# Halo tokens read channel-major, normalised without transposes, in a hybrid attention and pooling layer on eight cores

## What is computed

```python
h = rms_norm(x, norm_gain)                       # x * rsqrt(mean(x*x)) * gain
q, k, v, z_attn, u_pool, z_pool, gates = split(h @ w_in)      # 2048 x 16384
# attention: 3 groups of 8 heads, (window, dilation) = (128,1), (512,4), (2048,16)
#   q, k normalised per head, rope on 32 of 128 dims, softmax in the dilated window,
#   groups mixed by their softmax denominators
y_attn = (attn * silu(z_attn)) @ w_branch_attn
# pooling: trailing means over 2, 4, 8, 16 tokens minus the token, a map per group
y_pool = (pool * silu(z_pool)) @ w_branch_pool
out = x + (sigmoid(g_attn) * y_attn + sigmoid(g_pool) * y_pool) @ w_out
```

## Time and profile before

| | us |
|---|---|
| median of three runs | 1601.21 (1600.38 to 1602.24) |
| the execution with the profile | 1585.82 |
| its span, slowest core (6) | 1584.3 |
| spans of the eight cores | 1573.4 to 1584.3 |

### The profile page before, as it was taken

One profiled execution on the slowest core, in us unless ns is written; L12 is line 12 of the kernel. 1 busy time (PEld: TensorE's weight loads), 2 busy tenths in 40 slices (PEclk: granted clock), 3 DMA queues, 4 the chain that ended last, 5 costly groups with the idle time before them and its releaser, 6 DMA issues.

```text
span 1584.3 us, 27008 instructions; the slowest of 8 cores (1573.4 to 1584.3 us)
## 1 busy us (share of the span) xinstructions
PE 1549.4 (98%) x10200; PEld 934.9 (59%) x10200; DVE 640.2 (40%) x839; ACT 602.4 (38%) x985; POOL 86.9 (5%) x168
## 2 busy tenths in 40 slices
PE   6899999999999999999999999999999999999998
PEld 4555668746874846848656864856544444444443
DVE  5677723165514445543165515454522111113221
ACT  4566535353434543455353435553641111110000
POOL 0000000000000000000000000000000101000000
PEclk9989999999999999999999999999999999999999
DMA  9798441123131143241123131143544565542893
GB/s 244 185 237 209 97 90 32 28 51 73 33 54 34 35 75 71 38 78 32 28 52 73 32 54 34 35 86 61 123 77 85 105 106 98 89 80 40 189 224 120
DMA packets 42929, 138.04 MB, mean 87 GB/s; under 512 B 7025, under 2 KB 8049, under 8 KB 39537
## 3 DMA queue, kind: packets, MB, share of 16 engines
q0 software_dynamic: 23552, 85.58, 32.1%
q1 hardware_dynamic: 14498, 42.29, 8.4%
q10 hardware_dynamic: 4752, 8.44, 1.9%
HBM read 206.86 MB, written 10.49 MB: 137 GB/s over the span
## 4 chain that ended last, share of the span: by engine, by line
PE 93%; DMA 3%; DVE 2%; ACT 1%; issue 1%; SPq 0%; DVEq 0%; ACTq 0%; POOLq 0%
PE p_pp L464 77%; PE p_pnd L464 6%; PE p_psc L464 5%; PE p_pS L464 4%; DMA s_xt<-xh 1%; DMA pt_spill<-s_pt 1%; DMA s_wr<-w_in 1%; PE p_pnd L568 1%; DVE s_ub L475 1%; ACT s_xn L545 0%; ACT s_rr L468 0%; DVE s_xn L479 0%; DVE s_hTo L574 0%; DVE s_aT L479 0%; ACT s_hTh L472 0%
## 5 line engine op out<-in xcount | busy, mean ns | idle before, releaser
L464 PE MATMUL p_pp<-s_hTo,s_wr 128*128 128x512 bf16 (+4 forms) x3616 | 769.7, 367 | 9.5 <-DMA s_wr<-w_in 5.3
L464 PEld LDWEIGHTS p_pp<-s_hTo,s_wr 128*128 128x128 bf16 x3616 | 343.6, 99 | 370.9 <-issue 26.6
L479 DVE SCALAR_TENSOR_TENSOR s_kS<-p_pp,s_cst,s_rr 128x512 bf16<-128x512 f32 (+1 forms) x96 | 94.7, 986 | 273.4 <-ACT s_rr L468 267.4
L464 PE MATMUL p_pp<-s_wr,s_hTo 128*128 128x256 bf16 x1536 | 175.4, 273 | 0.0
L464 PEld LDWEIGHTS p_pp<-s_wr,s_hTo 128*128 128x128 bf16 x1536 | 160.7, 118 | 6.4
L464 PE MATMUL p_pp<-s_wr,s_hTh 128*128 128x256 bf16 x1344 | 159.5, 273 | 0.0
L464 PE MATMUL p_pp<-s_hTh,s_wr 128*128 128x512 bf16 (+1 forms) x768 | 155.7, 353 | 0.0
L468 ACT ACTIVATE s_rr<-p_pS 128x512 f32<-128x512 f32 x144 | 83.6, 580 | 181.5 <-PE p_pS L464 174.1
L464 PEld LDWEIGHTS p_pp<-s_wr,s_hTh 128*128 128x128 bf16 x1344 | 145.3, 136 | 1.9
L468 ACT ACTIVATE s_rr<-s_rr 128x512 f32<-128x512 f32 x208 | 128.5, 618 | 19.1 <-ACT s_rr L468 0.4
L487 POOL DMA_DIRECT2D s_wr<-w_in x128 | 67.6, 529 | 1219.2 <-PE p_pp L464 764.0
(11 more groups left out here) (75 smaller groups left out, 1205.0 us busy)
## 6 DMA issues: line engine op xcount, KB each, us to landing
s_wr<-w_in POOLq DMA_DIRECT2D x128, 512.0 KB, 5.5
s_xt<-xh SPq DMA_DIRECT2D x23, 1024.0 KB, 10.8
s_wr<-w_y POOLq DMA_DIRECT2D x16, 512.0 KB, 5.5
s_wo<-w_out POOLq DMA_DIRECT2D x16, 512.0 KB, 8.6
s_xr<-xh ACTq DMA_DIRECT2D x32, 256.0 KB, 7.8
out<-s_ob SPq DMA_DIRECT2D x32, 256.0 KB, 6.5
pt_spill<-s_pt SPq DMA_DIRECT2D x8, 256.0 KB, 6.6
s_pT<-pt_spill SPq DMA_DIRECT2D x1, 2048.0 KB, 12.9
```

Source lines behind the costliest of these rows:

```text
L464: S.op("pe", lambda t: t.matmul(out, lhsT=lhsT, rhs=rhs, start=start, stop=stop), reads=reads, writes=writes, cost=n / 2400.0 + 0.0025)
L479: S.op("dve", lambda v: v.scalar_tensor_tensor(out=out, in0=in0, scalar=scalar, in1=in1, op0=op0, op1=op1), reads=reads, writes=writes, co ...
```

## The change

The host also hands over the halo with channels on the partitions (`xg`: 20 pieces, each 128 channels x 4 x 384 tokens in f32, 768 KB). The tokens before 1920 are treated in five groups of 384 (`H_T0`: 1536 first, then 0, 384, 768, 1152). For a group (`h_task`) 16 squares of 384 columns are made on ScalarE, 15 adds of 384 columns in f32 on GpSimd bring them to one tile `acc`, one f32 matmul against ones (`onesf`) sums over the partitions and leaves the sum in all of them, Ln and Exp on ScalarE make the scale `rb`, and 16 products of 384 columns on VectorE (x times gain's column, times `rb`) write `hTh`. The tile-wise halo tasks, with their 240 transposes and 30 copies, are gone.

The first group must be done before the first V; the other four may go on beside the first V and the first K and Q (`end_halo`). For this the SBUF zones are laid out anew: the tiles that the first attention unit takes lie behind the x pieces. The masks and the third part of the rope table are loaded in `end_halo`, the other two parts where the whole table was. Weight blocks are issued up to three blocks ahead (`prefetch`), since GpSimd's queue now also has adds in it. The planner gets one modelled DMA channel of 290 GB/s for all large transfers, and per task its own margin and the engines whose lateness counts. The x loads of the own tokens stay as they were.

```diff
@@ -94,8 +97,11 @@
                 at = max(at, d.end + 0.1)
         if o.isdma:
             self.T[eng] = at + 0.1
-            self.chan[eng] = max(self.chan[eng], at + 1.5) + kb / (270.0 if kb >= 1024 else 540.0)
-            o.end = self.chan[eng] + 0.7
+            if kb >= 512:
+                self.bulk = max(self.bulk, at + 1.5) + kb / 290.0
+                o.end = self.bulk + 0.7
+            else:
+                o.end = at + 2.2 + kb / 540.0
         else:
             self.T[eng] = at + cost
             o.end = at + cost + (0.25 if eng == "pe" else 0.05)
...
@@ -205,10 +211,12 @@
 
 
 class Cond:
-    __slots__ = ("reads", "writes", "rings", "after", "heavy")
-
-    def __init__(self, reads=(), writes=(), rings=(), after=(), heavy=0.0):
+    __slots__ = ("reads", "writes", "rings", "after", "heavy", "margin", "on")
+
+    def __init__(self, reads=(), writes=(), rings=(), after=(), heavy=0.0, margin=0.6, on=("dve", "act")):
         self.heavy = heavy
...
@@ -282,9 +289,9 @@
                     self.step(t)
                     break
             else:
-                late = max(T["dve"], T["act"]) - T["pe"]
                 for t in self.live:
-                    if t.cond.heavy and late <= t.cond.heavy and self.ready(t):
+                    c = t.cond
+                    if c.heavy and max(T[e] for e in c.on) - T["pe"] <= max(c.heavy, self.floor) and self.ready(t):
                         self.step(t)
                         break
                 else:
...
+        zq_end = zQ.at
         xn_t = [zA.put(f"xn{i}", [128, D], BF16) for i in range(2)]
         gb = zA.put("gb", [128, D], F32)
         UW = PRE + TOWN
         grow = place("gr", [1, D], F32, at=aT_at)
         onef = place("of", [1, 128], F32, at=aT_at + 4 * D)
         uext0 = [zA.put(f"ua{i}", [128, UW], F32) for i in range(2)]
-        xt_t.append(place("xt3", [128, D], F32, at=zA.at))
...
@@ -488,8 +505,24 @@
                 "p (k c) -> p k c", k=KC)), behind=behind, writes=[B_wr[i]], dsem=f"dw{i}", kb=1024)
             return i
 
-        def load_wblock(col0, behind=()):
-            return load_w(w_in, col0, behind)
+        G0 = SEQ_G[0][0] * 1024
+        plan = ([CU, CU + 128, CZP, CZP + 128]
+                + [c + 256 * q + 128 * i for q in (1, 2, 3) for c in (CU, CZP) for i in (0, 1)]
+                + [CV + G0, CV + G0 + 128, CK + G0, CQ + G0, CK + G0 + 128, CQ + G0 + 128])
+        issued, taken = [], [0]
+
+        def prefetch(upto, behind=()):
+            while len(issued) < min(upto, len(plan)):
+                issued.append(load_w(w_in, plan[len(issued)], behind))
+
+        def load_wblock(col0, ahead=3):
+            n = taken[0]
+            taken[0] += 1
+            if n >= len(plan):
+                return load_w(w_in, col0)
+            assert plan[n] == col0
+            prefetch(n + ahead + 1)
+            return issued[n]
 
         B_gr, B_of = Buf("gr"), Buf("of")
         S.op("sp", lambda s: s.dma_start(out=grow[:], in_=gain), writes=[B_gr], dsem="dc1", kb=8)
...
+
+        load_early([x_op[0]])
+        load_early([x_op[1]])
+
+        XLATE = (5.0, 2.0, 2.0, 2.0, 2.0)
+        B_xq = [Buf(f"xq{i}") for i in range(6)]
+        XQ = (3, 2, 0, 1, 4, 5)
+        nq = [0]
+
+        def issue_q():
+            q = nq[0]
+            if q == 20:
+                return
+            nq[0] += 1
+            i = XQ[q % 6]
+            S.op("sp", lambda s: s.dma_start(out=xq_t[i][:], in_=xg[q * 128:(q + 1) * 128, :].rearrange(
+                "p (k t) -> p k t", k=4)), writes=[B_xq[i]], dsem=f"dq{i}", kb=8 * HT // 4)
+
         tp_t = [p[:, :].bitcast(BF16) for p in pnd_t]
 
         slot = {}
...
-            if j < 9:
-                slot[j] = xn.take("x")
+            slot[j] = xn.take("x")
             xi, ni, c0 = loaded[j], slot[j], 3 * j
             stt(xn_t[ni][:], xt_t[xi][:], stat[:, c0 + 2:c0 + 3], gb[:], ALU.mult, ALU.mult, 2048,
                 [xt.B[xi], B_st[j], B_gb] + bx, [xn.B[ni]], cost=2.35)
             if bx:
                 inherit(xt.B[xi], bx)
-            nx = j + 4 if j < 7 else j + 3
-            if j != 7 and nx < 24:
-                issue_x(nx)
+            if j < 5:
+                issue_x(j + 4)
+            if j == 6:
+                inherit(B_xq[3], [xt.B[2]])
+                inherit(B_xq[2], [xt.B[1], xt.B[2]])
+                issue_q()
+                issue_q()
+            if j == 8:
+                inherit(B_xq[0], [xt.B[0]])
+                inherit(B_xq[1], [xt.B[0], xt.B[1]])
+                issue_q()
+                issue_q()
 
         def x_turn(j, half):
...
@@ -583,35 +640,55 @@
                 vcopy(hTh[:, ks, THALO - 128:THALO - 16], i_ap[:, :, 16:128], 896, [pnd.B[pi]], [B_hH[15]])
             pnd.free(pi)
 
-        def x_task(j):
-            ti = tiles[j][1]
+        sf = Ring(sf_t, "sf")
+        B_acc, B_rb, B_of2 = Buf("acc"), Buf("rb"), Buf("onesf")
+
+        def padd(out, in0, in1, n, reads, writes):
+            S.op("pool", lambda g: g.tensor_tensor(out=out, in0=in0, in1=in1, op=ALU.add), reads=reads,
+                 writes=writes, cost=0.1 + n * 0.0022)
+
+        def h_task(gi):
+            t0 = H_T0[gi]
+            Bh = [B_hH[t0 // 128 + t] for t in range(HT // 128)]
 
             def gen(me):
-                yield Cond(after=[tile_front[j - 1]])
-                yield Cond(reads=[xt.B[loaded[j]]], rings=[xn], heavy=XLATE)
-                x_square(j, [])
-                x_scale(j, [])
-                xn.owner[slot[j]] = me
-                tile_front[j].done = True
-                for half in range(2):
-                    yield Cond(reads=[xn.B[slot[j]], B_id], rings=[pnd], heavy=XLATE)
-                    pi = x_turn(j, half)
-                    ks = slice(half * 8, half * 8 + 8)
-                    o_ap = hTh[:, ks, ti * 128:ti * 128 + 128]
-                    i_ap = tp_t[pi].rearrange("p (k c) -> p k c", c=128)
-                    if half == 0:
-                        acopy(o_ap, i_ap, 1024, [pnd.B[pi]], [B_hH[ti]])
+                yield Cond(after=[h_front[gi - 1]] if gi else [])
+                for kc in range(KC):
+                    xi = XQ[(4 * gi + kc // 4) % 6]
+                    yield Cond(reads=[B_xq[xi]], rings=[sf], heavy=XLATE[gi], on=("act", "pool"), margin=2.0 if kc % 4 == 0 else 0.6)
+                    si = sf.take(me)
+                    act(sf_t[si][:], xq_t[xi][:, kc % 4, :], AF.Square, HT, [B_xq[xi]], [sf.B[si]])
+                    if kc == 1:
+                        padd(acc[:], sf_t[s0][:], sf_t[si][:], HT, [sf.B[s0], sf.B[si]], [B_acc])
+                        sf.free(s0)
+                    elif kc:
+                        padd(acc[:], acc[:], sf_t[si][:], HT, [sf.B[si], B_acc], [B_acc])
+                    if kc:
+                        sf.free(si)
                     else:
-                        vcopy(o_ap, i_ap, 1024, [pnd.B[pi]], [B_hH[ti]])
-                    pnd.free(pi)
-                xn.free(slot[j])
+                        s0 = si
+                yield Cond(reads=[B_acc, B_of2], rings=[pnd], heavy=XLATE[gi], on=("act",))
+                pi = pnd.take(me)
+                mm(pnd_t[pi][:, 0:HT], onesf[:], acc[:], True, True, 4 * HT, [B_acc, B_of2], [pnd.B[pi]])
+                act(rb[:], pnd_t[pi][:, 0:HT], AF.Ln, HT, [pnd.B[pi]], [B_rb], bias=float(D * EPS))
+                act(rb[:], rb[:], AF.Exp, HT, [B_rb], [B_rb], scale=-0.5, bias=float(0.5 * np.log(D)))
+                pnd.free(pi)
+                h_front[gi].done = True
+                for q in range(4):
+                    xi = XQ[(4 * gi + q) % 6]
+                    yield Cond(reads=[B_rb], heavy=XLATE[gi], on=("dve",))
+                    for k in range(4):
+                        kc = 4 * q + k
+                        stt(hTh[:, kc, t0:t0 + HT], xq_t[xi][:, k, :], cst[:, C_GN + kc:C_GN + kc + 1], rb[:],
+                            ALU.mult, ALU.mult, HT, [B_xq[xi], B_rb, B_cst], Bh, cost=0.1 + HT * 0.0011)
+                    issue_q()
             return gen
 
         class Flag:
             def __init__(self):
                 self.done = False
 
-        tile_front = [Flag() for _ in range(24)]
+        h_front = [Flag() for _ in range(5)]
         B_pm = Buf("pm")
 
         def own_reads(lo, hi):
...
             if j == 1 or j == 2:
-                w01.append(load_wblock(CZP + (j - 1) * 128, [x_op[j + 2]]))
+                load_early([x_op[j + 2]])
             if j:
                 for blk in range(2):
                     u_group(blk, w01[blk], 128 * j - 128, 144 if j == 8 else 128)
             if j == 5 or j == 6:
                 z_early(j - 5, w01[2 + j - 5], 0)
+        inherit(B_xq[4], xn.B)
+        inherit(B_xq[5], [xn.B[1], B_gb])
+        inherit(sf.B[0], [B_gb])
+        inherit(sf.B[1], [B_gb])
+        issue_q()
+        issue_q()
+        S.op("dve", lambda v: v.memset(onesf[:], 1.0), writes=[B_of2])
```

(49 more changed lines are left out.)

82 lines of the change are left out of this document (46 added, 36 removed).

## The result

| | before | after |
|---|---|---|
| median, us | 1601.18 (5 runs, 1600.38 to 1602.24) | 1630.47 (5 runs, 1612.91 to 1638.04) |
| execution with the profile, us | 1585.82 | 1612.91 |

The ratio is 1.0157 (95% interval 1.0099 to 1.0214): slower by 1.6%, where 1589 us and faster had been forecast; the median of 1630.47 us also lies above the range of 1584 to 1620. The ratio comes from undisturbed runs alone, the medians in the table from all of them. A second timing of the same kernel on another chip gave 1.0146 (1.0129 to 1.0162), which is the figure that the experiments are compared with.

A forecast was written before the change was run, and what follows sets the result against it. TensorE, busy for 98%, bounds the kernel; time can be gained only in the 114 us before the first V. -13.5 + 3.4 - 5.7 + 3.5 = -12.3 us, from the median 1588.9, forecast 1589 us; range 1584 to 1620.

The forecast's parts named there:

- the add at 0.94: GpSimd, 384 columns: the planner's 0.94 us, between 0.53 and 1.24; 15 adds are 14.2 us a group, 70.5 in all.
- Even: VectorE before the first V: 42.5 us of products and copies go, 80 products of 384 columns come at 41.8 us.
- first rival: Before V, GpSimd and VectorE can't read at the same time: 17 us longer, 1618 us; chance 3 in 10.
- Transposes: TensorE before V: 30 halves of eight go, 0.45 us each, all on the path: -13.5 us.
- f32 matmuls: TensorE: five of 384 columns come, 0.67 us each at the high clock: +3.4 us, at most 6.7.
- one long stall and its clock gone, nothing late but x and adds: TensorE before V: 3.6 us stall and 2.1 of low clock go, -5.7; late adds 2.5 and late x 1, +3.5.
- The weights themselves: no cost.: Weights are issued three blocks (some 20 us) ahead against 5.5 us to land: no cost.
- VectorE's product, 0.52: VectorE, 384 columns at 1.1 ns a column: 0.52 us; 80 products, 41.8 us.
- GpSimd's lateness: TensorE's f32 matmuls wait for `acc`, 0.5 us a group after the margin: 2.5 us for five.
- break-even without contention: GpSimd's adds: the gain of 12.3 us is used up at 0.16 us more an add, 1.10 us.
- The second rival: GpSimd's chain of adds is slower by itself, 1.24 us an add: about 1606 us; chance 13 in 100.
- ScalarE, masks and table at no cost: ScalarE: 43 us of new work for 48 gone, no cost; masks and table, issued behind first K and Q, no cost.

The follow-up runs named there:

- the control: The changed kernel timed again with no edit, on another chip: 1606.01 us, 1.0146 of the kernel before.
- the sum on TensorE: Changed kernel without GpSimd adds: squares in bf16, summed by 16 matmuls of ones for a group; 1587.93 us, 1.0030 of the kernel before.
- the run with measured costs: Changed kernel with only the planner's costs changed (add 1.2, product 0.87, DMA issue on GpSimd 0.53): 1612.32 us, 1.0182 of the kernel before.

## Why the prediction was wrong

**The step that failed.** The prediction took the add at 0.94 and the product at 0.52 as if each engine ran alone, and wrote "Even" for VectorE. They don't run alone: an add on GpSimd and an instruction of VectorE with both operands in SBUF hold each other up. That was its first rival, at 0.30 and 1618 us (+17); +25 came by the first ratio and +22.3 in the control. Shown by two pairs of runs: 384 against 8 columns (1.0146 against 1.0003; product 901 against 635, pooling sum 1544 against 1240), and the scale in SBUF against PSUM (901 against 612 beside the same adds). The Trainium skill (SBUF — State Buffer, Who interferes with whom) states just this, and that an instruction of VectorE with at most one input in SBUF doesn't contend; the rows here agree with it (749 ns with and without adds for the product that reads PSUM). The argument against it, that weight issues keep 0.53 us beside any work, was none: they read no tiles, as the text itself said.

**Where the rival was off.** It added 64 us of adds and 38 of products to 32 of pooling sums and came to +17, too little. V starts 9.5 us later than before in the control, and the rest of its 22.3 us lies behind V, where the rival had nothing. It put TensorE's waits at the f32 matmuls and at banks; in the change's order it is nearly only the banks.

**The sum, by its terms.** For the adds of 8 columns the terms can be read. Transposes −13.5, as forecast; f32 matmuls 5 x 0.64 = 3.2 (from 210.26 to 210.90 us in the control), forecast 3.4; both right. Waits of TensorE between 60 and 300 us, those for `s_hTo` left out: 5.3 + 4.8 + 2.0 + 0.8 + 0.2 = 13.1, before 5.3: +7.8. The matmuls behind the three longest waits take, by the distances of their starts, 2.2, 2.5 and 1.2 us more than the same counts at the full clock (from 80.28 to 81.40 us four in 1.12, elsewhere 0.60). Before it is 2.9: the prediction counted 2.1 and left out the six matmuls from 115.84 to 117.99 us, 0.8 above the full clock. +3.0. −13.5 + 3.2 + 7.8 + 3.0 = +0.5; measured +0.05, as near as two cores of two executions can be compared. So "one long stall and its clock gone, nothing late but x and adds" (−5.7 + 3.5 = −2.2) is the second step that failed, with +10.8 in its place: without long adds two other waits take the stall's place. The control has −10.3 from TensorE's own work and waits of 30.9 (+25.6). Behind five of its eight waits matmuls are slowed in the same way, by 1.7, 2.3, 1.7, 1.9 and 1.6 us, 9.2 in all (+6.3). That is +21.6; measured +22.3.

**"The weights themselves: no cost."** Wrong by 4.8 us and 2.2 for the clock behind it. The first pooling block's weights compete with six pieces of x issued ahead. Shown by the two kernels in which three pieces wait for them: the wait is gone in both.

**VectorE's product, 0.52.** It takes 0.617 with GpSimd still. The line through 1024 and 2048 columns has a fixed part of 0.10 us in it, and the short product lies another 0.1 above that line; 80 x 0.1 = 8 us. Why, no run here shows. The planner has the same 0.52 and so ends a group earlier on paper than on the chip, which may be one reason for the burst; with the sum on TensorE the burst is absent with 0.52 too. Right costs alone aren't enough, by the run with measured costs: there the waits mostly move.

**GpSimd's lateness.** Add alone 0.99 us, a little over the 0.94 taken; break-even without contention was put at 1.10. The second rival (1.24 by itself, products at 0.52) didn't come: a uniform add and a free product is not what the rows show. The f32 matmuls wait for `acc` in the control not at all, forecast 2.5 us.

**ScalarE, masks and table at no cost.** No wait for masks or table is among those above; right. For ScalarE it is not quite so: TensorE waits for a square in front of a bank's reading, 3.1 us once in the control, 0.8 with adds of 8 columns and 2.9 in the sum on TensorE, and a square takes 516 ns, forecast 480.

**What stays open.** Why the clock stood near 0.8 from 85 to 235 us on six cores in the first profiled execution, and not in the control. And how the 1.4% splits between VectorE's longer work, the adds' lengthening and their length by itself (0.99 us alone, which the plan had nearly right): the scale in PSUM takes away 0.7 points, pooling sums with one operand in PSUM were not tried, and no run has whole adds that nothing on VectorE lengthens.

## What to carry to other kernels

Before work is put on an idle GpSimd, list what VectorE does in the same stretch and where its operands lie: with two in SBUF both engines' times lengthen, and the idle engine isn't free; put one operand into PSUM or sum on TensorE. An engine that issues weights should do nothing else, or each issue waits for its queue. And when a step gets shorter, look at what was just in time behind it: here the late weights and the forced last group ate all of 12 us, and holding back transfers that nobody needed yet gave 0.2 to 0.3 points in the two kernels in which it was tried.
